# A hybrid decoder step on one core: states of three heads kept for later, and one head's products moved among the experts

## What is computed

```python
# mixer: projections of the normalized rows, then two branches
q, k = rotary(q), rotary(k) * (RET_DK ** -0.5)      # 4 heads, DK = 256, DV = 512
r, ret_new = retention_chunkwise(q, k, v, state)    # ret_new: one (256, 512) state per head and sequence
r = r * rsqrt(mean(r * r) + eps)                    # the normalization per head
o_b = (silu(g) * r) @ w_b
o_a = (cb * short_conv(cc * ch)) @ w_a
h = x + (sigmoid(ga) * o_a + sigmoid(gb) * o_b) @ w_o
# experts: top 4 of 32, 1024 -> 2 * 1024 -> 1024
h = h + sum(gate * (((clip(up) + 1) * min(g, 7) * sigmoid(1.702 * min(g, 7))) @ w2 + b2))
```

## Time and profile before

| what | us |
|---|---|
| median of the runs | 1426.85 |
| the profiled execution | 1426.69 |
| its span | 1425.1 |
| PE busy | 1353.2 (95%) |
| DVE, ACT, POOL busy | 387.4, 252.3, 94.2 |
| bytes moved | 519.94 MB, mean 365 GB/s |
| the chain that ended last | PE 71%, DMA 26% |

### The profile page before, as it was taken

The page is one execution under the profiler, slowest core; times in us unless marked ns, Lnnn a source line. Parts: engine busy times, 40 slices in busy tenths (PEclk is TensorE's granted clock), DMA queues, the critical chain, the costliest instruction groups (busy, mean ns, idle before and its releaser), DMA issues.

```text
span 1425.1 us, 17289 instructions
## 1 busy us (share of the span) xinstructions
PE 1353.2 (95%) x7193; PEld 704.2 (49%) x7193; DVE 387.4 (27%) x711; ACT 252.3 (18%) x375; POOL 94.2 (7%) x163
## 2 busy tenths in 40 slices
PE   8999999999999999999989989889899898998997
PEld 6667668788887543443333334333333333332342
DVE  4235443642501331221221212212121122111223
ACT  1233343321000431111111101111011111101112
POOL 1122212210000210000000000000000000000000
PEclk9999999999999999999999999999999999999999
DMA  9987879874433589999999999999999999999997
GB/s 349 373 317 276 306 250 344 284 269 156 154 127 155 222 376 428 434 429 430 433 431 432 431 431 432 431 431 433 430 431 433 431 430 434 430 430 435 423 428 293
DMA packets 43298, 519.94 MB, mean 365 GB/s; under 512 B 5194, under 2 KB 5754, under 8 KB 21460
## 3 DMA queue, kind: packets, MB, share of 16 engines
q1 hardware_dynamic: 29136, 471.67, 79.1%
q0 software_dynamic: 12576, 44.62, 9.1%
q10 hardware_dynamic: 1540, 2.99, 0.5%
HBM read 497.63 MB, written 21.67 MB: 364 GB/s over the span
## 4 chain that ended last, share of the span: by engine, by line
PE 71%; DMA 26%; DVE 1%; SPq 1%; issue 0%; ACT 0%; DVEq 0%; ACTq 0%
PE bank L1846 24%; PE bank L1533 23%; DMA arena<-in_w_pairs 15%; DMA ring<-in_w_pairs 12%; PE bank L1811 4%; PE bank L1581 4%; PE bank L1797 3%; PE bank L1898 2%; PE bank L1676 2%; PE bank L1550 1%; SPq L632 1%; PE bank L1642 1%; PE bank L1844 1%; PE bank L1807 1%; PE bank L1875 1%; PE bank L1863 1%
## 5 line engine op out<-in xcount | busy, mean ns | idle before, releaser
L1846 PE MATMUL bank<-ring,arena 128*64 128x512 f32 x1536 | 348.4, 606 | 34.7 <-DMA ring<-in_w_pairs 34.7
L1533 PE MATMUL bank<-arena,ring 128*128 128x264 f32 x1472 | 335.7, 388 | 0.0
L1533 PEld LDWEIGHTS bank<-arena,ring 128*128 128x128 f32 x1472 | 277.5, 190 | 52.0 <-issue 6.0
L1846 PEld LDWEIGHTS bank<-ring,arena 128*64 128x64 f32 x1536 | 112.5, 139 | 247.7 <-issue 229.2
L1898 PE MATMUL bank<-ring,arena 128*64 128x512 f32 x768 | 172.6, 595 | 3.1 <-DMA ring<-in_w_pairs 3.0
L1846 PE MATMUL bank<-arena 128*64 128x512 f32 x512 | 118.4, 610 | 13.2 <-DMA arena<-in_w_pairs 13.2
L1898 PEld LDWEIGHTS bank<-ring,arena 128*64 128x64 f32 x768 | 55.1, 137 | 101.4 <-issue 99.6
L1463 DVE TENSOR_SCALAR arena<-bank 128x512 f32<-128x512 f32 x32 | 22.1, 691 | 272.5 <-PE bank L1846 272.5
L1846 PEld LDWEIGHTS bank<-arena 128*64 128x64 f32 x512 | 37.0, 140 | 87.8 <-issue 87.8
L1482 DVE COPY arena<-bank 64x512 f32<-64x512 f32 x32 | 21.9, 683 | 181.4 <-PE bank L1898 181.4
L1453 DVE TENSOR_TENSOR hs<-hs,bank 128x256 f32<-128x256 f32 x16 | 6.7, 421 | 225.3 <-PE bank L1807 225.3
(11 more groups left out here) (241 smaller groups left out, 995.5 us busy)
## 6 DMA issues: line engine op xcount, KB each, us to landing
ring<-in_w_pairs SPq DMA_DIRECT2D x59, 4096.0 KB, 28.9
arena<-in_w_pairs SPq DMA_DIRECT2D x19, 4096.0 KB, 27.1
ring<-in_w_mixer SPq DMA_DIRECT2D x58, 1024.0 KB, 8.6
ring<-in_w_pairs SPq DMA_DIRECT2D x26, 2048.0 KB, 12.7
arena<-in_state_ret POOLq DMA_DIRECT2D x32, 512.0 KB, 7.4
out_ret_sample<-arena POOLq DMA_DIRECT2D x32, 512.0 KB, 6.2
arena<-in_w_pairs SPq DMA_DIRECT2D x8, 2048.0 KB, 16.2
arena<-v_decode POOLq DMA_DIRECT2D x32, 256.0 KB, 6.9
```

Of the source, the lines that this page charges most:

```text
L1533: ins = pe.matmul(bank[:, 0:T], weight(n + k // 4, k % 4)[:, 128 * j:128 * (j + 1)], rhs[:, k, :], start=k == 0, stop=k == KD * groups - 1)
L1846: ins = pe.matmul(out, xgT[:, k, 64 * e:64 * (e + 1)], held(n, 2 * D * (k % W1_KS) + c), start=False, stop=k == KD - 1)
```

## The change

`DEFERRED` becomes (0, 1, 2): heads 0, 1 and 2 are kept, head 3's state is made in the mixer, straight behind its output, with its key turn in bank 7 just ahead of it and its gate projections behind. Head 0 is saved as before (values and turned keys). Of heads 1 and 2 the rotated keys are saved as they are, so their key turns leave the mixer; PE turns them later: head 1's in the middle of expert 0's up layer of the first pair, head 2's in the second pair. The `ss` of a decode head is not placed behind the third column of a q or k projection. The decode columns `qv` get a third buffer.

In the first pair head 1's products stand between the halves of the second up layer, where the gather was, and the gather goes behind that layer; head 2's products stand in the second pair, ahead of its down layers, in banks 0 and 1. ACT's first two pairs are written out, with the evictions in them. POOL loads head 2's values into the decode rows' place of `hx` once these are copied. Head 0's state is written from ACT before the experts, and DVE waits for that write before its loop.

```diff
-DEFERRED = (2, 3)
+DEFERRED = (0, 1, 2)
...
-        main.extend([(("v", h, 2), 2.2), (("vs", h), 0.0), (("v", h, 0), 7.0), (("qs", h), 0.0), (("kt", h), 0.5),
-                     (("sc", h), 1.4), (("v", h, 1), 7.0)])
-        proj(("g", h))
-        main.append((("out", h), 2.7))
-        main.append((("save", h), 0.0) if h in DEFERRED else (("st", h), 3.6))
+        main.extend([(("v", h, 2), 2.2), (("vs", h), 0.0), (("v", h, 0), 7.0), (("qs", h), 0.0)])
+        if h == 0:
+            main.append((("kt", h), 1.0))
+        main.extend([(("sc", h), 1.4), (("v", h, 1), 7.0)])
+        if h in DEFERRED:
+            proj(("g", h))
+            main.extend([(("out", h), 2.7), (("save", h), 0.0)])
+        else:
+            main.extend([(("kt", h), 1.0), (("out", h), 2.7), (("st", h), 3.6)])
...
-        if ends:
+        if ends and not (ends[0][0] == "ss" and event[0] == "proj" and event[1][0] in ("q", "k") and event[2] == 2):
...
+            use(event, TURN_BANK if event != ("kt", H - 1) else 7)
...
-    for i, h in enumerate(DEFERRED):
-        use(("st", h, 0), (0, 3)[i])
-        use(("st", h, 1), (4, 2)[i])
+    use(("st", 0, 0), 0)
+    use(("st", 0, 1), 4)
+    use(("kt", 1), 3)
+    use(("st", 1, 0), 6)
+    use(("st", 1, 1), 7)
...
+        values = [v_sb, view(14000, 2, DV), v_sb, view(14000, 2, DV)]
...
+        v_kept = [view(15072, 2, DV), view(17120, 2, DV), hx[:, 2, :].rearrange("p (t v) -> p t v", t=2)]
+        kT_kept = [None, [arena[:, 18144 + at:18144 + at + DK] for at in (0, DK)],
+                   [arena[:, 14784:14784 + DK], router[:, :, :].rearrange("p k e -> p (k e)")]]
+        k_kept = [view(16096, 2, DK), view(18656, 2, DK), view(19168, 2, DK)]
+        st_kept = [view(1024, 2, DV)] + [cst[:, C_COS + at:C_COS + at + D].rearrange("p (k v) -> p k v", k=2) for at in (D, 0)]
...
-            for i in range(len(DEFERRED)):
-                pool.dma_start(v_kept[i], v_kept_dram[i]).then_inc(kept_in, 16)
-                pool.dma_start(k_kept[i], k_kept_dram[i]).then_inc(kept_in, 16)
+            pool.dma_start(v_kept[0], v_kept_dram[0]).then_inc(kept_in[0], 16)
+            pool.dma_start(k_kept[0], k_kept_dram[0]).then_inc(kept_in[0], 16)
+            pool.dma_start(v_kept[1], v_kept_dram[1]).then_inc(kept_in[1], 16)
+            for t in range(2):
+                pool.dma_start(kT_kept[1][t], k_kept_dram[1][:, t, :]).then_inc(kept_in[1], 16)
+            pool.dma_start(kT_kept[2][0], k_kept_dram[2][:, 0, :]).then_inc(kept_in[2], 16)
...
+            pool.wait_ge(hs_ready, 4)
+            pool.dma_start(v_kept[2], v_kept_dram[2]).then_inc(kept_in[2], 16)
+            was_filled(pool, "last_logits")
+            pool.dma_start(kT_kept[2][1], k_kept_dram[2][:, 1, :]).then_inc(kept_in[2], 16)
...
+                        if t == 0 and h >= 2:
+
+                            was_filled(ac, ("out", h - 2, 1))
...
-                    was_read(ac, ("kt", h))
-                    i = DEFERRED.index(h)
-                    ac.dma_start(v_kept_dram[i], values[h]).then_inc(saved, 16)
-                    ac.dma_start(k_kept_dram[i], ktok[:, :, :]).then_inc(saved, 16)
+                    ac.dma_start(v_kept_dram[h], values[h]).then_inc(saved, 16)
+                    if h == 0:
+                        was_read(ac, ("kt", h))
+                        ac.dma_start(k_kept_dram[h], ktok[:, :, :]).then_inc(saved, 16)
+                    else:
+                        hh = 2 * (h % 2)
+                        ac.wait_ge(qk_ready, 8 * (h // 2 + 1))
+                        ac.dma_start(k_kept_dram[h], kT[:, hh:hh + 2, 0:LP]).then_inc(saved, 16)
...
+            def ktok_half(i, t, bank):
+
+                return ac.activation(k_kept[i][:, t, :], bank[:, DK * t:DK * (t + 1)], ACT.Copy,
...
+            ac.wait_ge(kept_read, 2)
+            ac.dma_start(o["ret_prompt"][0, 0, 0].rearrange("(k p) v -> p k v", p=128), st_kept[0]).then_inc(st_out, 16)
...
+            bank = read(ac, ("kt", 1))
+            for t in range(2):
+                ins = ktok_half(1, t, bank)
+            empties(ins, ("kt", 1))
...
+            def expert_pair(r, pair, first=False, late=False):
+                it = r * PAIRS + pair
+                ac.wait_ge(pg_turned, it + (1 + PRIMED))
+                ac.wait_ge(pad_zero, 1)
+                ac.activation(pgT[:, 0:T], psum[TURN_BANKS[0]][:, 0:T], ACT.Copy).then_inc(pgT_ready, 1)
+                for e in range(2):
+                    ac.wait_ge(g_clip, 2 * it + e + 1)
+                    ac.activation(sig[:, e, :], gcl[:, e, :], ACT.Sigmoid, scale=ALPHA).then_inc(sig_ready, 1)
+                    if late and e == 1:
+                        for g in range(2):
+                            ac.wait_ge(late_state, 2 * r + g + 1)
+                            ac.activation(st_kept[2][:, g, :], psum[LATE_BANKS[g]][:, :], ACT.Copy).then_inc(late_read, 1)
+                    if e == 0 and not first:
+                        low_half(it + 1)
+                    ac.wait_ge(act_turned, 2 * it + e + 1)
+                    ac.activation(actT[:, e, :], psum[TURN_BANKS[e]][:, :], ACT.Copy).then_inc(actT_ready, 1)
+                    if e == 0 and first:
+                        low_half(it + 1)
+                    if late and e == 0:
+                        ac.wait_ge(routed, 1)
+                        ac.wait_ge(kT_turned, r + 1)
+                        for t in range(2):
+                            ktok_half(2, t, psum[LATE_BANKS[1]]).then_inc(late_ktok, 1)
+                for e in range(2):
+                    ac.wait_ge(down_done, 2 * it + e + 1)
+                    ac.activation(ysb[SLOTS * e:SLOTS * (e + 1), 512:1024], psum[Y_BANKS[e]][64:128, :], ACT.Copy)\
+                        .then_inc(y_hi_ready, 1)
+
             with ac.Fori(0, rounds) as r:
-                with ac.Fori(0, PAIRS) as pair:
-                    it = r * PAIRS + pair
-                    ac.wait_ge(pg_turned, it + (1 + PRIMED))
...
+                        if (name, g, j) == ("k", 1, 1):
+                            v.wait_ge(saved, 64)
...
+            v.wait_ge(st_out, 32)
...
+            def turn_kept(i, bank):
+
+                for t in range(2):
+                    for half in range(2):
+                        ins = pe.transpose(bank[:, DK * t + 128 * half:DK * t + 128 * (half + 1)],
+                                           kT_kept[i][half][:, 128 * t:128 * (t + 1)], ident)
...
-                    first_layer(0, range(-1, KD))
+                    first_layer(0, range(-1, 4))
+                    pe.wait_ge(kept_in[1], 48)
                     pe.wait_ge(added, ADDS * it + ADDS)
-                    final_states(4, 8)
+                    fills(turn_kept(1, fill(pe, ("kt", 1))), ("kt", 1))
...
-                if first:
-                    pe.wait_ge(kept_read, 2 * len(DEFERRED))
-                    pe.wait_ge(rest_ready, len(SPLITS))
...
+                if first:
+                    was_read(pe, ("kt", 1))
                 first_layer(1, range(-1, 4))
-                gather(g + 1)
+                if first:
+                    final_states(1, 0, 4)
+                else:
+                    gather(g + 1)
                 pe.wait_ge(pgT_ready, it + 1)
                 turn_acts(0)
+                if alone:
+                    pe.wait_ge(kept_in[2], 48)
+                    turn_kept(2, psum[LATE_BANKS[1]]).then_inc(kT_turned, 1)
                 first_layer(1, range(4, KD))
+                if first:
+                    pe.wait_ge(kept_read, 4)
+                    pe.wait_ge(rest_ready, len(SPLITS))
+                    gather(g + 1)
+                if alone:
+                    pe.wait_ge(late_ktok, 2 * r + 2)
+                    for g in range(2):
+                        for t in range(2):
+                            ins = pe.matmul(psum[LATE_BANKS[g]][:, :], k_kept[2][:, t, 128 * g:128 * (g + 1)],
+                                            v_kept[2][:, t, :], start=t == 0, stop=t == 1)
+                        ins.then_inc(late_state, 1)
                 second_layer(0, range(0, 4))
                 turn_acts(1)
+                if alone:
+                    pe.wait_ge(late_read, 2 * r + 2)
                 second_layer(0, range(4, KD))
                 second_layer(1, range(0, KD))
 

```

More of the change, by code:

```diff
@@ L45 @@
 TURN_BANKS = (5, 3)
+LATE_BANKS = (0, 1)
 Y_BANKS = (4, 2)
@@ L279, in mixer_order @@
     for h in range(H - 2):
-        assert at["ss", h] < at["proj", ("g", h + 2), 0] and at["rsT", h] < at["qs", h + 2]
+        assert at["ss", h] < at["proj", ("g", h + 2), 0] and (h + 3 >= H or at["rsT", h] < at["qs", h + 3])
     return order
@@ L487, in build @@
         rT_ready, ctok_out, merged_ready = sem("rT_ready"), sem("ctok_out"), sem("merged_ready")
-        saved, kept_in, kept_read = sem("saved"), sem("kept_in"), sem("kept_read")
+        saved, kept_read = sem("saved"), sem("kept_read")
+        kept_in = [sem(f"kept_in{h}") for h in DEFERRED]
```

(38 more changed lines are left out.)

50 lines of the change are left out of this document (18 added, 32 removed).

## The result

| | before | after |
|---|---|---|
| median of 5 runs each, us | 1428.42 (1426.83 to 1429.3) | 1433.78 (1432.35 to 1435.14) |
| the profiled execution | 1426.69 | 1433.78 |
| its span | 1425.1 | 1432.0 |
| PE busy | 1353.2 | 1357.8 |
| ACT busy | 252.3 | 211.0 |

The ratio is 1.0037, with an interval of 1.0026 to 1.0048: the changed kernel is slower, by some 5 us. The forecast was 1427.4, 0.7 above the execution that it was built on and so next to no change, and its range ended at 1430.6. The measured time lies outside that range.

What follows compares the result with a forecast made beforehand. PE bounds mixer and router, DMA the late expert pairs, so the end depends on when PE reaches the first chunk and whether the stream runs dry. Mixer -3.5, between +0.2, queue +4.0 on 1426.69 gave 1427.4 us, range 1423.5 to 1430.6.

Steps and rivals of the forecast that it cites:

- State products, -3.5: Mixer: heads 0 and 1 lose their state product, head 3 gets one, 3.54 us each, so -3.5 us.
- Head 3's bank 7, +1.4: Mixer, head 3's attention output: PE waits for ACT's key halves in bank 7, +1.4 us, between 0 and 4.0.
- Its rival (1430.0): Head 3's bank 7: ACT stands ahead of the state scaling for its DMA, PE loses up to 4.0 us; chance 0.15.
- The decode wait, -0.5: Mixer: PE's 0.5 us wait for a decode row goes, as head 1's normalization now lands behind the last state product.
- What would show it: Signs: first up layer near 502.5, PE waits of 1.3 (head 3) and about 6 us (pair 0), DMA holes in pairs 0 and 1.
- Between mixer and pairs, +0.2: Ahead of the expert stream: late loads and state write, 2.6 us of DMA, fit into idle DMA; +0.2, between 0 and 2.6.
- PE's wait, 5.9: First pair, ahead of the turned activations: new 5.9 us wait behind ACT's state reads, 2.8 us net for the chunks behind.
- the slack of a 4 MB issue: Second pair, issue at 602.5: landing 18.5 less 12.8 us for an empty queue gives 5.7 us of slack.
- the largest excess alone counts: Expert stream: of the excesses over slack, 2.2 us at 539.0 and 4.2 at 602.5, only the larger counts; taken as +4.0.
- the wait costs nothing: Rival, first pair: ACT's chain is shorter or PE less late, the stream stays full, 1423.4 us; chance 0.20.
- One table load fewer: Rival, first pair: unrolling leaves one ACT table load, wait 4.6, loss 2.7, time 1426.1 us; chance 0.07.
- The slower case: Outcome slower than no change, by the head 3 bank 7 rival at 1430.0 us; chance 0.15.

Runs made afterwards that it cites:

- early_write_moved: The changed kernel with ACT's eviction of head 1's state behind the first sigmoid, plus head 0's state written behind the loops: 1425.83 us in one execution.
- wait_filled: The changed kernel with 25 unused bf16 products put into PE's wait ahead of the first pair's turned activations: 1431.57 us, ratio 1.0025.
- pair0_more: The kernel before with 17 unused bf16 products (3.6 us of PE) ahead of expert 0's turned activations in the first pair: 1433.11 us, ratio 1.0033.
- after_again: The changed kernel, nothing edited, profiled once more: 1433.62 us in one execution.

## Why the prediction was wrong, step by step

- **What bounds the kernel: right.** Stream and PE regimes are as described, and the end is the opening issue plus the length of the stream, 915.3 to 915.4 in the three traces of before.
- **State products, -3.5: right.** 7.07 to 3.44, start to start, -3.6.
- **Head 3's bank 7, +1.4: right in kind and nearly in size.** PE's waits at L1674 are 0.9 together. Attention outputs take 0.9 more and key turns 0.5 less, +0.4 net where -0.9 + 1.4 gave +0.5. The forecast's own counting gave a wait of 1.25, and its 1.4 has no reason beside it. Its rival (1430.0) did not happen: ACT goes from the decode product into the state scaling and the key without idle time, in the trace of after:

```profile
195.48 0.71 ACT L847 ACTIVATE arena<-arena 128x512 f32<-128x512 f32 x1
196.09 1.05 ACT L834 ACTIVATE arena<-arena 128x1024 f32<-128x1024 f32 x1
197.04 0.83 ACT L874 ACTIVATE arena<-bank,cst 128x256 f32<-128x256 f32 x2
```

- **The decode wait, -0.5: the wait went, the time did not.** The projections in which it was counted take 333.11 in place of 333.04, and scores and sums of squares 0.4 more; PE has a new wait of 0.2 for `rs_t`. The mixer nets -2.6, not -3.5. Where the rest of this 0.9 comes from, row by row, I have not settled. Of the planner's new order this much is shown: with the rule no value projection waits for its bank, as counted; without it one does, for 2.1 us.
- **What would show it:** the first up layer "near 502.5" starts at 504.3. Of these 1.8 us later than forecast, 0.9 is the start-up and 0.9 the mixer, so this sign misled: as it was written it points to the last rival (505), whose wait did not come. The wait of 5.5 and the hole behind it were plain. The second hole, forecast for pair 1, is not: the chunk of 594.6 lands 7.9 late and that of 602.5 8.5.
- **Between mixer and pairs, +0.2: right within 0.3** (51.22 to 51.14, and early_write_moved).
- **PE's wait, 5.9: right, 5.5.** Two table loads stayed in the first pair, and the sigmoid starts 0.02 us behind its load, so the drain that the Trainium skill gives (ScalarE: Activation LUTs, What ACT_TABLE_LOAD costs) is not seen after either.
- **First failed step: a wait was priced at its length.** "Turns the activations at 537.6 instead of 534.78 ... 2.8 us net for the chunks behind it" left out that PE comes out of the wait at half its clock, though the late pairs of before show it (719.47 above). This is 2.4 us in the trace of after, and 2.2 of it go when the wait is filled (wait_filled). The 12.9 us by which the chunk at 602.5 is late are 3.0 (order) + 2.4 (clock) + 3.3 (gather behind the layer) + 4.2 (head 2); forecast 9.9.
- **Second failed step: the slack of a 4 MB issue.** "4 MB would land after 12.8" was worked out by adding bytes at the full rate; dry, it is 14.1 in after and 13.5 to 14.6 over the traces. The slack of 5.7 was 4.4 in after, which is 1.3 us, and 3.9 to 5.0 by the others. The slack at 539.0 was wrong the other way (1.2, not 0.6), and the forecast's end did not rest on it. The stream so comes to 12.9 - 4.4 = 8.5, measured 8.7, in place of 4.2.
- **Also off: the largest excess alone counts.** In pair0_more a hole costs 1.2 us more than its excess, so the term for the queue was too small by its rule as well. In after this is 0.2.
- **The base.** After's start-up is 0.9 longer than that of the one execution that I built on.

The sum closes on the two profiled executions: stream +4.7 against the forecast, mixer +0.9, start-up +0.9, router -0.3, around the span +0.2: 6.4 us, which is 1433.8 - 1427.4.

As to the rivals: "the wait costs nothing" named the right place and the right condition, but the wait did not shrink. "One table load fewer" failed in the first pair, which keeps both. It came true behind it, where the DMA share is 1.00 with the loads and without: before had 16 loads ahead of pgT and 16 ahead of the sigmoid, after has one of each in all, and ACT's busy time fell from 252.3 to 211.0. The slower case had 0.15 and the wrong mechanism. The real one, ACT's state evictions ahead of the first sigmoid, stood in my sum as a term, and I let its price end at PE's idle time.

## What to carry to other kernels

In a stretch that DMA feeds, price a new wait of TensorE three times: its length, the work behind it at half the clock (the trace before the change may already show such waits, with what followed them), and how late the next loads are issued against the slack that their landing times show. Take that slack from the landing of the same size of load in a queue that has just run dry, not from bytes over rate, and allow for its scatter (13.5 to 14.6 us here). When products are moved between two dependent steps, move their evictions behind the activation that the next matmul waits for: here two instructions of 0.6 us decided between 0.4% slower and 0.2% faster. And cut executions at fixed points before believing one of them: start-up and router varied by some 1.6 us each, the mixer by 0.1, the stream by 0.1 in one kernel and by 0.9 over kernels with the same work in it.

## What the runs showed of the hardware that I had not expected

- A PE wait of 3.0 us lowered the granted clock to 0.50, as one of 5.5 did: the 32 matmuls behind took 8.78 and 8.93 us (8.27 in after_again), at 1.2 GHz for part of them, in place of 7.03. With 0.2 us idle there was no fall, and behind the 15 waits of 2.1 to 2.9 us in the late pairs of before the work was slow 7 times.
- The clock also falls with PE at work, behind a stretch of small products, in some executions of the same program and not in others: 5.38 in place of 3.68 us for one product, 1.7 us of the whole.
- A transfer of 2 MB lands after 7.2 to 7.9 us in a dry queue, one of 4 MB after 13.5 to 14.6.
- With the first two pairs written out, the table loads vanish from the later pairs as well: 32 become 2. It takes 38 us off ACT. No run has this change alone, so what it does to the time isn't measured.
